# The last gate tile of the SSM branch multiplied earlier, the paired products in the other PSUM banks, and the first k-steps with their three products in another order

## What is computed

```python
h = rmsnorm(x, norm_pre) * (1.0 + scale[:, None, :]) + shift[:, None, :]
proj = h @ w_in
u_pool, z_pool, u_ssm, z_ssm, g_pool, g_ssm = jnp.split(proj, list(IN_SPLITS), axis=-1)
y_pool = causal_pool_mixer(u_pool, pool_w, pool_scale) * jax.nn.silu(z_pool)
y_ssm = s5_mixer(u_ssm, a_re, a_im, log_dt, b_re, b_im, c_re, c_im, d_skip,
                 glu_w, glu_b) * jax.nn.silu(z_ssm)
merged = (jax.nn.sigmoid(g_pool) * (y_pool @ w_branch_pool)
          + jax.nn.sigmoid(g_ssm) * (y_ssm @ w_branch_ssm))
out = merged @ w_out
return x + gate[:, None, :] * rmsnorm(out, norm_post)
```

## Time and profile before

| | us |
|---|---|
| median of 3 runs | 933.82 |
| lowest, highest | 933.70, 934.33 |
| the profiled execution, its own time | 933.93 |
| its span in the trace | 932.1 |
| PE busy | 909.8 (98%) |
| DVE busy | 726.2 (78%) |
| ACT busy | 389.0 (42%) |

### The profile page before, as it was taken

The page is one execution under the profiler, slowest core; times in us unless marked ns, Lnnn a source line. Parts: engine busy times, 40 slices in busy tenths (PEclk is TensorE's granted clock), DMA queues, the critical chain, the costliest instruction groups (busy, mean ns, idle before and its releaser), DMA issues.

```text
span 932.1 us, 11810 instructions
## 1 busy us (share of the span) xinstructions
PE 909.8 (98%) x4312; PEld 763.3 (82%) x4312; DVE 726.2 (78%) x1057; ACT 389.0 (42%) x534; POOL 45.3 (5%) x82
## 2 busy tenths in 40 slices
PE   3999999999999999999999999999999999999996
PEld 3888888888888888888888888888888888887885
DVE  5988899887777888546789589948468786679977
ACT  5841353343444444344544353623144460136443
POOL 0019900000000000000000000000000000000000
PEclk9999999999999999999999999999999999999999
DMA  9843265545455364437799676476355268454233
GB/s 351 313 142 106 118 228 184 163 159 158 161 195 184 143 225 175 180 75 199 191 265 244 132 198 156 132 247 231 114 226 203 95 225 320 182 198 154 76 106 135
DMA packets 97449, 169.85 MB, mean 182 GB/s; under 512 B 38768, under 2 KB 55280, under 8 KB 97392
## 3 DMA queue, kind: packets, MB, share of 16 engines
q1 hardware_dynamic: 87600, 164.55, 54.1%
q10 hardware_dynamic: 9792, 4.56, 1.9%
HBM read 121.88 MB, written 47.19 MB: 181 GB/s over the span
## 4 chain that ended last, share of the span: by engine, by line
PE 96%; DVE 1%; ACT 1%; DMA 1%; issue 0%; ACTq 0%; DVEq 0%
PE ps L2537 41%; PE ps L2691 32%; PE psb L2691 13%; PE ps L2762 2%; PE psb L2742 2%; PE psb L2751 2%; PE psa L2730 2%; PE psa L2617 1%; PE psa L2537 1%; DMA par_are<-in_a_re 1%; PE psb L2617 0%; PE psb L2567 0%; ACT gt L1196 0%; DVE mod_out L1747 0%; PE psa L2567 0%
## 5 line engine op out<-in xcount | busy, mean ns | idle before, releaser
L2537 PE MATMUL ps<-bop,w_hi 128*128 128x512 f32 x864 | 232.2, 391 | 0.8 <-DVE bop L1789 0.8
L2537 PEld LDWEIGHTS ps<-bop,w_hi 128*128 128x128 f32 x864 | 161.2, 188 | 33.7 <-issue 0.9
L2537 PE MATMUL ps<-bop,w_lo 128*128 128x512 f32 x432 | 133.0, 389 | 0.0
L2537 PEld LDWEIGHTS ps<-bop,w_lo 128*128 128x128 f32 x432 | 81.1, 188 | 17.0
L2691 PE MATMUL ps<-bop,r_hi 128*128 128x512 f32 x272 | 83.7, 389 | 0.0
L1743 DVE TENSOR_TENSOR w_lo<-raw,w_hi 128x1024 fp32r<-128x1024 f32 x35 | 43.4, 1239 | 37.8 <-ACT w_hi L1182 37.5
L1182 ACT ACTIVATE w_hi<-raw 128x1024 fp32r<-128x1024 f32 x35 | 36.9, 1053 | 76.6 <-PE ps L2537 68.4
L2691 PEld LDWEIGHTS ps<-bop,r_hi 128*128 128x128 f32 x272 | 51.1, 188 | 10.6
L2691 PE MATMUL ps<-t_hi,r_hi 128*128 128x512 f32 x140 | 55.1, 393 | 0.0
L2691 PE MATMUL ps<-t_hi,r_lo 128*128 128x512 f32 x140 | 54.6, 390 | 0.0
L2691 PE MATMUL ps<-t_lo,r_hi 128*128 128x512 f32 x140 | 54.5, 389 | 0.0
(11 more groups left out here) (464 smaller groups left out, 1889.0 us busy)
## 6 DMA issues: line engine op xcount, KB each, us to landing
raw<-in_wstream SPq DMA_DIRECT2D x36, 512.0 KB, 5.4
pair_raw<-in_wstream SPq DMA_DIRECT2D x30, 512.0 KB, 4.2
ada<-in_w_ada SPq DMA_DIRECT2D x16, 512.0 KB, 11.3
x_tok<-in_x SPq DMA_DIRECT2D x8, 512.0 KB, 7.0
gs_d<-gt SPq DMA_DIRECT2D x8, 512.0 KB, 4.9
win_d<-win_new SPq DMA_DIRECT2D x8, 512.0 KB, 2.7
wout_d<-wout_new SPq DMA_DIRECT2D x8, 512.0 KB, 3.8
wout<-wout_d SPq DMA_DIRECT2D x8, 512.0 KB, 4.8
```

Source lines behind the costliest of these rows:

```text
L2537: last = mm(ps[slot(u)][:, f * HALF:f * HALF + HALF], a[:, k, :], b(k, f), start=k == order[0] and q == 0, stop=k == order[-1] and q == 2)
```

## The change

- `("zs", 7)` leaves turn 0 and becomes the tenth and last of `FIRST`. Its weights are loaded, split, multiplied, passed through SiLU into `gt[1]` and stored there, each at a new place in its engine's program; the two waits that its old place needed go.
- Since `FIRST` has one tile more, the weights of `("up", 0)` change buffers and its PSUM tile is the other one; from `("up", 1)` on both are as before.
- The pairs' `side` is turned over: a pair that used `gt[1]`, `rt[1]` and the half banks of that side now uses the others. Some waits at the seams follow: the first turn's product waits for `c11_done` 14 in place of `c21_done` 13.
- In `step` the order of the three products is high weights by high `h`, low weights by high `h`, high weights by low `h`, and only the third waits for `h_done`; the first two wait for `h_hi_done`.

```diff
-FIRST = [("gs", n) for n in range(KT)] + [("zs", 0)]
+FIRST = [("gs", n) for n in range(KT)] + [("zs", 0), ("zs", 7)]
...
-FILL = {0: [("zs", 7)], 4: [("zp", 6)], 7: [("zp", 7)]}
+FILL = {4: [("zp", 6)], 7: [("zp", 7)]}
...
-    return (j + (j < NP)) % 2
+    return j % 2
...
             store_gs(6)
+            load_w(9)
             sp.wait_ge(coef_ready, 2)
...
-            sp.dma_start(zs_d[0], gt[0][:, :]).then_inc(zs_stored, 16)
+            sp.dma_start(zs_d[0], gt[0][:, :]).then_inc(zs_stored[0], 16)
+            sp.wait_ge(job_out[slot(("zs", 7))], evicted(("zs", 7)))
+            sp.dma_start(zs_d[7], gt[1][:, :]).then_inc(zs_stored[1], 16)
...
-                if m == 1:
-                    sp.wait_ge(job_out[slot(("zs", 7))], evicted(("zs", 7)))
-                    sp.dma_start(zs_d[7], zs_last).then_inc(zs_stored, 16)
...
             pair_high(0, P3)
+            act.wait_ge(gs_stored[1], 16 * 4)
+            evac(("zs", 7), gt[1][:, :], ACT.Silu)
             pair_high(0, P4)
...
             t_sums(3)
+            split_lo(9)
...
-                pe.wait_ge(h_done, k + 1)
-                last = k_step(u, k, *h)
+                pe.wait_ge(h_hi_done, k + 1)
+                hi, lo = (wx_hi, wx_lo) if n == 2 else (w_hi[n % 2], w_lo[n % 2])
+                for q, (a, part) in enumerate(((hi, h[0]), (lo, h[0]), (hi, h[1]))):
+                    if q == 2:
+                        pe.wait_ge(h_done, k + 1)
+                    for f in range(2):
+                        last = mm(ps[slot(u)][:, f * HALF:f * HALF + HALF], a[:, k, :], part(k, f),
+                                  start=k == 0 and q == 0, stop=k == KT - 1 and q == 2)
...
-            pe.wait_ge(c21_done, NP - 1)
+            pe.wait_ge(c11_done, NP)
             pe.wait_ge(c12_done, NP - 1)
...
-                    pe.wait_ge(c11_done, NP)
+                    pe.wait_ge(c21_done, NP)
                     pe.wait_ge(c12_done, NP)
```

More of the change, by code:

```diff
@@ L410, in build @@
         vta = ssm("vta", [P, GB, CH, SG])
-        zp_t = [t[:, :] for t in (gt[1], rt[1], gt[0], rt[0])]
+        zp_t = [t[:, :] for t in (gt[0], rt[0], gt[1], rt[1])]
         zp_t += [t[:, :, :].rearrange("p g c -> p (g c)") for t in (cos_pa, sin_pa)]
         zp_t += [vta[:, :, :, :].rearrange("p g t h -> p (g t h)"), pu[:, :, :].rearrange("p t c -> p (t c)")[:, 0:SEQ]]
-        zs_last = zp_t[6]
         pfix = ssm("pfix", [P, CH, 2])
@@ L532, in build @@
         gs_stored = two("gs_stored")
-        zs_stored = sem("zs_stored")
+        zs_stored = two("zs_stored")
         y_loaded = [sem(f"y_loaded{w}") for w in range(4)]
@@ L1058, in _ @@
             sp.wait_ge(in_lo_done, KT)
-            sp.wait_ge(zs_stored, 32)
+            for s in range(2):
+                sp.wait_ge(zs_stored[s], 16)
             sp.wait_ge(sq_ready, KT)
@@ L1298, in pair_high @@
                 elif o >= 4:
-                    act.wait_ge(mm_done, JOB[FIRST[-1 if o < 6 else -2]] + 1)
+                    act.wait_ge(mm_done, JOB[FIRST[-2 if o < 6 else -1]] + 1)
                 u = pair_weights(j)
@@ L1326, in copy_p1 @@
                     act.wait_ge(pair_stored[j % 2], 32 * (j // 2))
-                if j == 0:
-                    act.wait_ge(gs_stored[1], 16 * 4)
-                if j == 1:
-                    act.wait_ge(zs_stored, 16)
+                if j < 2:
+                    act.wait_ge(zs_stored[j], 16)
                 act.wait_ge(st_done, S_POS[j, P1] + 1)
@@ L1503, in _ @@
                 for u in FILL.get(m, ()):
-                    dst = zs_last if u[0] == "zs" else zp_t[u[1]]
-                    if u == ("zp", 6):
-                        act.wait_ge(zs_stored, 32)
-                    elif u == ("zp", 7):
+                    dst = zp_t[u[1]]
+                    if u == ("zp", 7):
                         act.wait_ge(pooled, KT)
@@ L1950, in pair_slot @@
                 elif o >= 4:
-                    dve.wait_ge(mm_done, JOB[FIRST[-1 if o < 6 else -2]] + 1)
+                    dve.wait_ge(mm_done, JOB[FIRST[-2 if o < 6 else -1]] + 1)
             def sum1(j):
@@ L2624, in half_product @@
                 if i == P1:
-                    if j == 0:
+                    if j == 1:
                         pe.wait_ge(job_out[0], SLOT[:len(FIRST)].count(0))
@@ L2653, in half_product @@
                     else:
-                        pe.wait_ge(job_out[j], SLOT[:len(FIRST)].count(j))
+                        pe.wait_ge(job_out[1 - j], SLOT[:len(FIRST)].count(1 - j))
                 elif i == P7:
```

## The result

| | before | after |
|---|---|---|
| median, us | 933.88 (14 runs) | 936.05 (14 runs) |
| lowest, highest | 933.54, 935.05 | 935.06, 937.47 |
| the profiled execution | 933.93 | 936.07 |
| its span | 932.1 | 934.3 |

Both were timed again side by side: the ratio is 1.0022, with a 95% interval of 1.0015 to 1.0030, so the changed kernel is slower by 2.2 us. The profiled executions differ by 2.14 us. The forecast was 936.3, from a sum of +2.4 us.

What follows compares the result with a forecast made beforehand. PE was taken as the bound, by the number of matmuls and their pace. 2.85 us of wait for `win` less 0.4 at the start gave +2.4 on 933.82, so 936.3 us, range 934.2 to 938.2.

Steps and rivals of the forecast that it cites:

- The place and the sign: Turn 1, second `part_b`: PE waits for `win` near 446.6, not at `part_states`, and the kernel gets slower; chance 0.62.
- The start, 0.4 us: First k-steps: the first ends 0.95 to 1.0 us earlier, but (1, 0) waits for `h_ready`, leaving 0.4 us won.
- low weights come late: Rival at the first k-step: it can't start on the high part for lack of low weights; costs 0.4 us, giving 936.7.
- The seam, nothing: End of the first products, near 129: moved `zs` 7 and turned banks cost nothing, with 2.8 us of cover.
- The wait for `win`, 2.85 us: At `part_b(1)`: `win` lands at 438.93, PE is there 10.88 us sooner and waits 2.8 us, plus 0.05 for the signal.
- It keeps its distance: SP's queue before `win` of turn 1 starts at a fixed point, contains nothing of `zs` 7, so its timing stays.
- I count no wait: `part_taps(1)` in turn 2: SP issues its `taps` until 454.5, PE arrives at 457.0; 2.5 us to land, no wait.
- Since PE never waits afterwards nothing gives it back: After turn 1: from turn 2 on the order is that of before, so the 2.8 us wait stays in the total.
- The early landing: Rival in turn 1: `win` lands early, PE stalls 1.25 us at `part_states(0)` instead; 934.7 us, chance 0.17.
- The change doesn't do what it says: Rival at the start: the first k-step can't start on the high part; costs the 0.4 us, giving 936.7.
- The second gap: Rival in turn 2: late `taps` cost 1 us or so; chance 0.11 together with the falling clock.
- The fall of the clock: Rival after the turn 1 gap: PE's clock drops, at most 1.9 us, giving 938.2; chance 0.11 together with a second gap.

Runs made afterwards that it cites:

- e3: The changed kernel with SP's load of `win` for turn 1 issued ahead of the loads of `u_in`; 935.50 us, ratio 1.0015 against the kernel before.
- e1: The kernel before with only the new order of the three products in the first k-steps; 933.89 us, ratio 0.9996 against the kernel before.
- e2: The changed kernel with the old order of products, so only the tile moved and banks turned; 936.63 us, ratio 1.0026 against the kernel before.
- e4: The changed kernel with the tables of turn 2 issued after that turn's `win`, `u_in`, `taps` and `wout`; 937.79 us, ratio 1.0038 against the kernel before.
- e12: The same kernel as e11, profiled once more; 941.05 us (1 run).
- e6: The changed kernel with the 64 loads of `taps` issued by POOL in place of SP; 948.39 us, ratio 1.0149 against the kernel before.
- e11: The changed kernel with the load `raw` that followed `win` issued ahead of it in turn 0; 939.09 us, ratio 1.0054 against the kernel before.
- e7: The changed kernel with `taps` issued by POOL and `part_states(0)` inside the product of `up` 2; 947.51 us, ratio 1.0129 against the kernel before.

## Why the prediction was right, and where it was not

**The place and the sign: right.** PE waits at the second `part_b` for `win<-win_d`, near 446.5; `sq` of turn 0 ends at 451.19, which is 440.8 in the prediction's clock plus 10.88 less 0.5; it is early enough for `part_states(0)`, and late by 1.22 us when `win` comes early (e3). "PE waits nowhere else" is what failed, below.

**The start, 0.4 us: right** in size and cause by e1, 0.44 from the first matmul. That the changed kernel's profile shows nearly the same, -0.38, is luck: its first matmul came 0.23 us sooner by itself, its transposes took 0.7 us longer, so its first k-step began at 25.81 and not near 25.2 (e1: 24.85), and counted from the first matmul only 0.15 us is won there. The wait for `h_full` ahead of (1, 0) that the prediction announced is not in this profile, since PE came late enough. The step "low weights come late" was a rival for the first k-step; the new short wait for `w_lo` (0.3 us in e1) stands at the step (1, 0), and costs nothing that can be seen, since `h_full` ends at 28.57 there and PE begins at 28.66.

**The seam, nothing: off by 0.15 us**, and on the good side. Between the start and turn 0 the change wins from -0.38 to -0.53; in e1, without the moved tile, the start gain of 0.71 at the step (1, 0) shrinks to 0.35, and PE's only new wait there is 0.2 us for a copy of ACT in the first pair. In e2, with the moved tile alone, the lead grows from 0.23 to 0.43 instead. That the moved tile gives ACT and DVE more room there fits both, but no run shows it by itself.

**The wait for `win`, 2.85 us: mis-sized, 1.73.** Two numbers went into it. "It keeps its distance" held, but not the lengths of the issues: eight `taps` and eight `u_in` took 4.93 + 4.18 us in place of 5.24 + 5.37. By that alone SP would be 1.5 us sooner, but other loads ahead of it take back 1 us, and `win` was issued 0.5 us sooner. The landing took 5.7 us and not 6.3. Both were within the bounds of the prediction (0.3 to 4.3). The estimate of 5.1 us that the prediction worked out from the Trainium skill (DMA: Bandwidth & Descriptors, Latency and other measured facts) was off by as much as the row's 6.3, 0.6 us below and 0.6 above; its wait of 1.6 us is near the measured 1.73 only because `win` was also issued sooner. The eight loads of the changed kernel spread from 3.7 to 8.5 us, so neither is a value to rely on.

**"I count no wait" for turn 2: wrong, 0.8 us.** The step put the last `taps` 2.5 us ahead of PE. Its end of the issue was right (454.5 in that clock, 464.3 in the trace less 10.35 is 454.0). But it left 2.5 us for the last ones to land, from a PE that was thought 1.1 us later; and they took longer. The last one took 3.2 us, where before, at the same place, it took 2.0; the last two `u_in` took 5.5 us, where before they took 3.3. The window from 455 to 465 shows why, first before, then after:

```profile
455.00:465.00 10.00, 10.00 (x54) 8.56 (x53) 8.36 (x14) 3.61 (x4) 0.00 (x0) 1.00 0.66 165
```

```profile
455.00:465.00 10.00, 9.81 (x44) 7.81 (x44) 8.26 (x14) 4.66 (x6) 0.00 (x0) 1.00 1.00 227
```

The DMA share rises from 0.66 to 1.00: the last tables were issued 4.3 us ahead of the first `u_in` before, and are 0.7 us ahead now, with `win` between. In e4, without the tables, the same eight `u_in` took 2.5 us.

So the sum, +2.4, came near the measured +2.14 because two errors of opposite sign met: 1.1 us too much for `win`, 0.8 too little for turn 2, and 0.15 for the seam. They are not independent: a later start in turn 1 gives the loads of turn 2 as much more time, as e2 shows. That the sum is off by only 0.3 us is in part luck. One bound was also added up wrong: a landing of 7.8 us with a gain of 0.1 gives 938.1, not 937.8.

**"Since PE never waits afterwards nothing gives it back": the right number, the wrong picture.** The prediction saw one load in one place of a queue. The runs that take this wait away keep 1.2 to 2.0 of the 2.1 us, since DVE got only 7.5 us quicker where PE skips 10.88, and is late by itself by 2.9 us in turn 1. The prediction had looked at DVE for `sq` of turn 0 only, and not one turn further.

**The rivals.** The early landing, made by hand in e3, gave the stall of 1.22 us that was worked out, but ended at +1.6 and not +0.9, for the same reason. "The change doesn't do what it says" fell. The second gap came, at 0.8 us, "1 us or so". The fall of the clock did not happen in the profile (1.00 in the windows after the gap), but was dismissed too lightly: with a row of 2.36 us it happened and cost 1.6. Its price was read rightly, 1.9 us at most from the first transposes: they are as slow as the matmuls behind the gap of e12 (last section), and 1.6, 2.5 and 2.9 us were measured. The wait that the prediction expected, 2.8 us, lies between the ones for which it was seen and not seen. The warning against gaps of about 3 us in the Trainium skill (TensorE: Matmul & The Clock Gate, Goal table of Why this matters for your kernels) is borne out by e12 (4.30 us), while e6 lost the clock behind less (2.36) and e11 kept it behind 3.01. Three of the 14 executions of the changed kernel took 937.2 to 937.5 us, where the 14 of before stayed under 935.1. Their mean granted clock is 0.996 or 0.997, that of the other eleven 0.997 or 0.998: a fall of the clock would fit, but the difference is too small to show it, and they have no trace.

## What to carry to other kernels

When a piece of PE's work moves away, what it covered is not one load but the sum of work of every engine between two points: take from the trace each engine's idle time in the stretch, and where it is less than the product that goes (here 8.4 us of idle time on DVE against 10.88), expect the difference to come back, in this turn or a later one. Removing the wait that the profile then showed mostly moved it here (from turn 1 to turns 2 and 4): look for the timestamp that stays fixed while the waits move, here the end of `sq`. And a landing time is a property of what else is in flight, so a margin of a microsecond or two read from one row isn't one when the neighbours of that load change.

No version beat the kernel before by an amount that the timing shows; the new order of the products alone (e1) is the best, by 0.35 us in the trace.

## What I had not expected of the hardware

- With the 64 loads of `taps` issued by POOL, SP's loads landed 1.3 to 2.2 us later by the median, and the whole kernel was 8 us slower (942.27 against 934.22 us beside it), though there were fewer packets (81,328 on the queues of SP and POOL against 87,600).
- PE's clock fell behind a gap of 2.36 us in one run and stayed through one of 3.01 us in another. The same kernel took 936.4 and 941.1 us in two profiled executions, by 1.8 us of a later start at `part_b(1)` and 2.9 us of clock.
- The first transposes, 24 matmuls by the profile's count, took from 4.2 to 5.3 us in the profiles, 0.5 to 0.64 of the later pace, in stretches whose row of the granted clock says 1.00. But one of them takes as long as one of the matmuls of e12 in its stretch at a granted clock of 0.50, 421 ns, where later ones take 275 ns (the loads of weights take 333 ns in both, and 192 later). So they ran at the pace of the lower clock, though the row of the granted clock doesn't show it there. What differs between the profiles is how long that lasts: in the changed kernel all 16 of the row below took 421 ns, in e7 the median is 275. A window of the changed kernel, its transposes there, and the matmuls of e12:

```profile
14.50:19.00 4.50, 4.50 (x22) 4.50 (x23) 3.28 (x14) 4.07 (x7) 0.00 (x0) 1.00 1.03 386
```

```profile
L2566 PE MATMUL ps<-diag,x_tok x16: 421/421/421, 16.1 to 19.3; 128*128 128x128 f32 x16
```

```profile
L2738 PE MATMUL psa<-u_in,win x16: 420/421/579, 451.3 to 454.6; 128*128 128x128 f32 x16
```
